# A two-block transformer on one core: the norms between the stages of the first block

## The reference, cut to what matters

```python
def rmsnorm(x, g):
    xf = x.astype(jnp.float32)
    y = xf * lax.rsqrt(jnp.mean(xf * xf, axis=-1, keepdims=True) + RMS_EPS)
    return (y * g.astype(jnp.float32)).astype(x.dtype)

for i in range(DEPTH):                                  # DEPTH = 2
    g = norm_g[i]
    f1 = swiglu(rmsnorm(h, g[0]), ffn_w_gate[i, 0], ffn_w_up[i, 0], ffn_w_down[i, 0])
    h = h + FFN_RES * rmsnorm(f1, g[1])
    hn = rmsnorm(h, g[2])
    m = neighborhood_attention(hn, ...)                 # i = 0; diff_attention for i = 1
    h = h + rmsnorm(m, g[3])
    f2 = swiglu(rmsnorm(h, g[4]), ffn_w_gate[i, 1], ffn_w_up[i, 1], ffn_w_down[i, 1])
    h = h + FFN_RES * rmsnorm(f2, g[5])
```

## Time and profile before

| | us |
|---|---|
| median of 3 runs | 2372.04 (2369.4 to 2373.62) |
| profiled execution | 2367.97 |
| its span | 2366.1 |
| PE busy in the span | 2271.9 (96%) |
| DVE busy | 1615.5 (68%) |
| ACT busy | 1040.3 (44%) |
| POOL busy | 110.4 (5%) |

### The profile page before, as it was taken

The page is one execution under the profiler, slowest core; times in us unless marked ns, Lnnn a source line. Parts: engine busy times, 40 slices in busy tenths (PEclk is TensorE's granted clock), DMA queues, the critical chain, the costliest instruction groups (busy, mean ns, idle before and its releaser), DMA issues. The chain is left out here.

```text
span 2366.1 us, 46054 instructions
## 1 busy us (share of the span) xinstructions
PE 2271.9 (96%) x18286; PEld 2132.5 (90%) x18286; DVE 1615.5 (68%) x3000; ACT 1040.3 (44%) x1688; POOL 110.4 (5%) x42
## 2 busy tenths in 40 slices
PE   7999999999999998999799998989999999999997
PEld 7999789999999887999789997989999998888886
DVE  5665567664765466766476667689889975777775
ACT  5443455443544345544363435434444444333333
POOL 0000000000000000000000000069300000000000
PEclk9999999999999999999898998999999999999999
DMA  5563434554455342456332225535444445555553
GB/s 192 171 200 118 169 109 135 177 193 147 143 174 197 122 145 81 152 187 205 113 129 73 82 82 172 167 118 169 142 141 138 142 161 169 188 194 192 191 194 133
DMA packets 99245, 361.12 MB, mean 153 GB/s; under 512 B 11496, under 2 KB 15224, under 8 KB 98944
## 3 DMA queue, kind: packets, MB, share of 16 engines
q1 hardware_dynamic: 99072, 358.64, 45.8%
HBM read 357.55 MB, written 1.05 MB: 152 GB/s over the span
## 5 line engine op out<-in xcount | busy, mean ns | idle before, releaser
L876 DVE TENSOR_TENSOR w_lo<-ring,w_hi 128x1024 fp32r<-128x1024 f32 (+1 forms) x304 | 397.6, 1308 | 241.3 <-ACT w_hi L693 241.0
L693 ACT ACTIVATE w_hi<-ring 128x1024 fp32r<-128x1024 f32 (+1 forms) x304 | 341.3, 1125 | 401.8 <-PE ps L427 364.2
L427 PE MATMUL ps<-x_hi,w_hi 128*128 128x272 f32 (+1 forms) x1664 | 488.2, 293 | 18.0 <-DVE w_lo L876 16.5
L427 PE MATMUL ps<-x_hi,w_lo 128*128 128x272 f32 (+1 forms) x1664 | 479.1, 288 | 0.0
L427 PE MATMUL ps<-x_lo,w_hi 128*128 128x272 f32 (+1 forms) x1664 | 478.4, 288 | 0.0
L427 PEld LDWEIGHTS ps<-x_hi,w_hi 128*128 128x128 f32 x1664 | 314.5, 189 | 25.2 <-issue 10.7
L427 PEld LDWEIGHTS ps<-x_lo,w_hi 128*128 128x128 f32 x1664 | 314.1, 189 | 1.0
L427 PEld LDWEIGHTS ps<-x_hi,w_lo 128*128 128x128 f32 x1664 | 314.5, 189 | 0.0
L234 ACT ACTIVATE v_gated_hi<-ring 128x1024 fp32r<-128x1024 f32 x128 | 135.9, 1062 | 214.7 <-PE ps L2863 214.0
L2650 PE MATMUL ps<-tok_hi,u_mid_hi 128*128 128x256 f32 x736 | 213.6, 290 | 1.3 <-POOL u_mid_lo L240 1.3
L2650 PE MATMUL ps<-tok_hi,u_mid_lo 128*128 128x256 f32 x736 | 208.1, 283 | 0.0
(11 more groups left out here) (479 smaller groups left out, 5029.8 us busy)
## 6 DMA issues: line engine op xcount, KB each, us to landing
ring<-in_gate_up SPq DMA_DIRECT2D x176, 512.0 KB, 3.3
ring<-in_peer_v SPq DMA_DIRECT2D x128, 512.0 KB, 3.2
ring<-in_peer_u_mid SPq DMA_DIRECT2D x92, 512.0 KB, 3.3
ring<-in_down SPq DMA_DIRECT2D x64, 704.0 KB, 4.1
ring<-in_w_in SPq DMA_DIRECT2D x46, 512.0 KB, 3.3
ring<-in_peer_u_early SPq DMA_DIRECT2D x36, 512.0 KB, 3.2
ring<-in_project SPq DMA_DIRECT2D x32, 512.0 KB, 4.1
ring<-in_na_qk SPq DMA_DIRECT2D x16, 512.0 KB, 3.8
```

The source lines that it names most:

```text
L427: mm = nc.tensor.matmul(ps[:, bank, 0:ntok], parts[left][:, slot, t * P:(t + 1) * P], rhs[right][:, k, 0:ntok], start=start and n == 0, st ...
L693: A.activation(parts[0][:, n % SLOTS, 0:width[n]], ring[:, n % SLOTS, 0:width[n]], ACT.Copy).then_inc(hi_done.sem, 1)
L876: V.tensor_tensor(parts[1][:, n % SLOTS, 0:width[n]], ring[:, n % SLOTS, 0:width[n]], parts[0][:, n % SLOTS, 0:width[n]].bitcast(F32), ALU ...
```

## The change

The boundary is computed in another way.

- **No reciprocal ahead of the products.** Instead of h + y/s (s is `std` of y), the boundary makes h' = s*h + y, which is s times the new stream. x is made of h'. Its norm cancels s, if the epsilon is multiplied by the square of s: ACT makes that square into `inv_h` (`eps_squared`), and it is added to the sum of squares. The factor s*h of tiles 0 and 1 is made by DVE (`raise_rows`, `h_raised_first`), of tiles 2 to 7 by GpSimd (`raise_rest`). Later, GpSimd multiplies h' by 1/s to bring the stream back (`lower`, `h_back`); the reciprocal that this needs (`inverse`) stands on DVE behind the last `x_lo`. At b = 6 the stream is made as before.
- **Sums of squares.** GpSimd adds the tiles of `sq` up element by element into tile 0 (`gather_y`: tiles 1 to 6; `gather_h`: the epsilon's term and tiles 1 to 7). PE multiplies by `ones` twice for a norm of y (`y_sum_most`, `y_sum_last`) and once for a norm of h, which stands behind item 3 in a feed-forward now.
- **The first tile of x.** PE starts with the products that need only `x_hi`, for three items (banks) in turn, and runs those with `x_lo` behind them.
- **Splits ahead.** At b = 0, 2, 3 and 5, two more weight items (4 and 5) are split in the boundary, and no longer in the loop. At b = 1 and 4 it stays three items.
- **keep_busy** runs 10 products, not 20.

The diff, cut to its core:

```diff
+        RAISED = range(1, 6)
+        FIRST_ROWS = 2
+        def raise_rows(eng, b, k):
+            if b == 5:
+                return eng.tensor_tensor(halves(h[:, k, :]), halves(h[:, k, :]), std[:, 0:SEQ].rearrange("p (b t) -> p b t", t=P), ALU.mult)
+            return eng.tensor_tensor(h[:, k, 0:T], h[:, k, 0:T], std[:, 0:T], ALU.mult)
+        def ahead_of(b):
+            return 3 if b in (1, 4) else 2
...
+            def y_sum_most(b):
+                pe.wait_ge(y_gathered, b)
+                nc.tensor.matmul(ps[:, 6, 0:stream(b)[1]], ones[:, :], sq[:, 0, 0:stream(b)[1]], start=True, stop=False)
+            def y_sum_last(b):
+                pe.wait_ge(y_squared, KD * b)
+                nc.tensor.matmul(ps[:, 6, 0:stream(b)[1]], ones[:, :], sq[:, KD - 1, 0:stream(b)[1]], start=False, stop=True).then_inc(y_summed, 1)
+            def h_sum(b):
+                pe.wait_ge(h_gathered, b + 1)
+                nc.tensor.matmul(ps[:, 7, 0:stream(b)[1]], ones[:, :], sq[:, 0, 0:stream(b)[1]], start=True, stop=True).then_inc(h_summed, 1)
             def keep_busy():
-                for _ in range(20):
+                for _ in range(10):
...
+            def first_side_by_side(n0, banks, ntok, b):
+                pe.wait_ge(x_hi, KD * b + 1)
+                for n, bank in enumerate(banks):
+                    pe.wait_ge(lo_done.sem, n0 + n + 1)
+                    for left in range(2):
+                        nc.tensor.matmul(ps[:, bank, 0:ntok], parts[left][:, (n0 + n) % SLOTS, 0:P], x[0][:, 0, 0:ntok], start=(left == 0), stop=False)
+                pe.wait_ge(x_lo, KD * b + 1)
+                for n, bank in enumerate(banks):
+                    nc.tensor.matmul(ps[:, bank, 0:ntok], parts[0][:, (n0 + n) % SLOTS, 0:P], x[1][:, 0, 0:ntok], start=False, stop=False)
...
-                for k in range(KD):
+                first_side_by_side(n0, (0, 1, 2), ntok, b)
+                for k in range(1, KD):
                     pe.wait_ge(x_lo, KD * b + k + 1)
                     side_by_side(n0, (0, 1, 2), k, ntok, x)
-                    if k:
-                        h_sum(b, k - 1)
-                h_sum(b, KD - 1)
                 for i in range(3, 2 * KF):
                     if i >= 6:
                         pe.wait_ge(taken, taken0 + i - 5)
                     whole_item(n0 + i, i % 6, ntok, x)
+                    if i == 3:
+                        h_sum(b)
...
-                    if side == 1 and m:
-                        y_sum(b + 1, m - 1)
-                y_sum(b + 1, KD - 1)
+                y_sum_most(b + 1)
+                y_sum_last(b + 1)
...
# ACT, boundary: behind the root of the sum for y, and ahead of the root for h
+                if b in RAISED:
+                    act.wait_ge(y_std, b)
...
+                        A.activation(inv_h[:, 0:T], std[:, 0:T], ACT.Square, scale=math.sqrt(EPS * D / P)).then_inc(eps_squared, 1)
...
-                if b in (1, 4):
-                    for n in range(n_next + 1, n_next + 4):
-                        split_hi(n)
+                for n in range(n_next + 1, n_next + 1 + ahead_of(b)):
+                    split_hi(n)
                 act.wait_ge(h_summed, b + 1)
+                if b:
+                    act.wait_ge(y_inv, b)
...
# DVE, boundary
                 def new_h(k):
-                    V.tensor_tensor(y[:, k, 0:ntok], y[:, k, 0:ntok], inv_y[:, 0:ntok], ALU.mult).then_inc(y_scaled, 1)
-                    dve.wait_ge(y_scaled, KD * (b - 1) + k + 1)
+                    if b == 6:
+                        V.tensor_tensor(y[:, k, 0:ntok], y[:, k, 0:ntok], inv_y[:, 0:ntok], ALU.mult).then_inc(y_scaled, 1)
+                        dve.wait_ge(y_scaled, k + 1)
+                    elif k < FIRST_ROWS:
+                        if b >= 2:
+                            dve.wait_ge(h_back, KD * (b - 2) + k + 1)
+                        raise_rows(V, b, k).then_inc(h_raised_first, 1)
+                        dve.wait_ge(h_raised_first, FIRST_ROWS * (b - 1) + k + 1)
+                    else:
+                        dve.wait_ge(h_raised, (KD - FIRST_ROWS) * (b - 1) + k - FIRST_ROWS + 1)
...
+                if b and b not in (1, 4):
+                    inverse()
+                for n in range(n_next + 1, n_next + 1 + ahead_of(b)):
+                    split_lo(n)
                 if b in (1, 4):
+                    inverse()
                 dve.wait_ge(h_std, b + 1)
                 V.reciprocal(inv_h[:, 0:ntok], std[:, 0:ntok]).then_inc(h_inv, 1)
...
+            def gather_y(b):
+                ntok = stream(b)[1]
+                for k in range(1, KD - 1):
+                    pool.wait_ge(y_squared, KD * (b - 1) + k + 1)
+                    if k > 1:
+                        pool.wait_ge(y_link, (KD - 3) * (b - 1) + k - 1)
+                    G.tensor_tensor(sq[:, 0, 0:ntok], sq[:, 0, 0:ntok], sq[:, k, 0:ntok], ALU.add).then_inc(y_link if k < KD - 2 else y_gathered, 1)
+            def raise_rest(b):
+                pool.wait_ge(y_std, b)
+                for k in range(FIRST_ROWS, KD):
+                    if b >= 2:
+                        pool.wait_ge(h_back, KD * (b - 2) + k + 1)
+                    raise_rows(G, b, k).then_inc(h_raised, 1)
+            def lower(b):
+                stem, ntok = stream(b)
+                pool.wait_ge(y_inv, b)
+                pool.wait_ge(x_lo, KD * (b + 1))
+                for k in range(KD):
+                    G.tensor_tensor(stem[:, k, 0:ntok], stem[:, k, 0:ntok], inv_y[:, 0:ntok], ALU.mult).then_inc(h_back, 1)
+            gather_h(0)
+            for b in range(1, 7):
+                gather_y(b)
+                if b in RAISED:
+                    raise_rest(b)
+                    gather_h(b)
+                    lower(b)
```

More of the change, by code:

```diff
@@ L502, in attention, with v_product @@
                         k = 2 * pair + t
-                        if side == 0:
+                        if side == 0 and k:
                             pe.wait_ge(x_lo, KD * b + k + 1)
-                        for tile, (t0, n) in enumerate(KEY_TILES):
-                            for term, (left, right) in enumerate(TERMS):
-                                mm = nc.tensor.matmul(ps[0:n, 3 * side + tile, :], x[left][:, k, t0:t0 + n],
-                                                      parts[right][:, (n0 + item) % SLOTS, 512 * t:512 * t + 512],
-                                                      start=(k == 0 and term == 0), stop=(k == KD - 1 and term == 2))
+                        def v_product(tile, left, right, start=False, stop=False):
+                            t0, n = KEY_TILES[tile]
+                            return nc.tensor.matmul(ps[0:n, 3 * side + tile, :], x[left][:, k, t0:t0 + n],
+                                                    parts[right][:, (n0 + item) % SLOTS, 512 * t:512 * t + 512], start=start, stop=stop)
+                        if item == 0 and k == 0:
+                            pe.wait_ge(x_hi, KD * b + 1)
+                            for tile in range(3):
+                                v_product(tile, 0, 0, start=True)
+                                v_product(tile, 0, 1)
+                            pe.wait_ge(x_lo, KD * b + 1)
+                            for tile in range(3):
+                                mm = v_product(tile, 1, 0)
+                        else:
+                            for tile in range(3):
+                                for term, (left, right) in enumerate(TERMS):
+                                    mm = v_product(tile, left, right, start=(k == 0 and term == 0), stop=(k == KD - 1 and term == 2))
                         if t == 1:
                             mm.then_inc(used, 1)
-                        if side == 0 and k:
-                            h_sum(b, k - 1)
                     if item == 3:
-                        h_sum(b, KD - 1)
+                        h_sum(b)
                     if item == 5:
@@ L671, in attention @@
                     whole_item(n0 + m, bank, ntok, o_parts)
-                    y_sum(b + 1, m - 3)
-                for m in range(KD - 3, KD):
-                    y_sum(b + 1, m)
+                y_sum_most(b + 1)
+                y_sum_last(b + 1)
                 pe.wait_ge(taken, taken0 + 3)
@@ L711, in boundary @@
                     return
+                if b in RAISED:
+                    act.wait_ge(y_std, b)
+                    if b == 5:
+                        A.activation(to_rows(inv_h[:, 0:SEQ]), by_columns(std[:, 0:SEQ]), ACT.Square, scale=math.sqrt(EPS * D / P)).then_inc(eps_squared, 1)
+                    else:
+                        A.activation(inv_h[:, 0:T], std[:, 0:T], ACT.Square, scale=math.sqrt(EPS * D / P)).then_inc(eps_squared, 1)
                 for k in range(KD):
@@ L737, in ffn @@
                 for i in range(2 * KF):
[L738 removed]
+                    if i >= 2:
+                        split_hi(n0 + i + 4)
                     j = i // 2
@@ L919, in boundary @@
```

(7 more changed lines are left out.)

59 lines of the change are left out of this document (43 added, 16 removed).

## The result

| | before | after |
|---|---|---|
| median of the runs | 2370.88 (2369.4 to 2373.62, 4 runs) | 2341.57 (2340.4 to 2343.38, 4 runs) |
| span of the profiled execution | 2366.1 | 2338.5 |
| PE busy | 2271.9 | 2235.8 |
| DVE busy | 1615.5 | 1641.7 |
| POOL busy | 110.4 | 253.8 |

The ratio is 0.9876, with a 95% interval of 0.9859 to 0.9893: 1.24% faster. The forecast was 2347, in a range of 2326 to 2362. By the profiled executions the gain is 27.6 us against the 25.2 of the sum.

A forecast was written before the change was run, and what follows sets the result against it. PE was taken as the bound, others setting the pace only in boundaries. Gains of 16.5 (sums of y), 3.9 (start), 4.8 (attention boundaries) and 0 (feed-forward boundaries) made 25.2 us, giving 2347, range 2326 to 2362.

The forecast's parts named there:

- The sums of y: Down-product stages of 6 sublayers: 36 products with `ones` at 0.46 us go off PE, 16.5 us gained.
- The price of GpSimd: A GpSimd instruction of 272 columns, shown in no earlier row, was taken to cost 0.75 us.
- The rival at 1.0 to 1.2: Boundaries: dearer GpSimd instructions lengthen DVE's chain; 2363 at 1.0, 2378 at 1.2; chances 0.04 (1.0 to 1.1), 0.04 (slower than before).
- an estimate of 0.84: GpSimd's instruction price by the skill's 4497 ns and the trace's 2.38; would shrink the gain from 25 to 19 us.
- The turns: Boundaries: of two DVE and GpSimd instructions with two SBUF inputs, one waits for the whole of the other.
- A pair: Boundaries: one DVE and one GpSimd instruction in turn cost 0.96 us, where DVE alone needs about 0.4.
- Boundaries into a feed-forward: Boundaries 2, 3, 5: first product 2.0, last `x_lo` 15.7, item 4 21.2 us behind the root; net gain about 0.
- the wait of 0.3 at item 6: Boundaries into a feed-forward: item 6 waits about 0.3 us for its `w_lo`, now behind first results, root and silu.
- Boundaries into an attention: Boundaries 1 and 4: item 4 of v starts at 21.9, before 24.3; gain 2.4 us each, 4.8 together.
- The start: At b = 0: fewer sums ahead of item 3 and no stall ahead of item 4; gain 3.9 us.
- The clock: Rival at boundaries 2, 3, 5: PE's granted clock falls, costing about 4 us at each, 2358; chance 0.12.
- a stall of 1.4: Ahead of item 4 in the kernel before: PE lost 1.4 us, which goes as splits run under item 3.

The follow-up runs named there:

- experiment 1: Kernel before with only the sums of squares of y changed: GpSimd adds squares 1 to 6, PE does 2 products with ones a sublayer; 2351.7, ratio 0.9925.
- Experiment 2: Kernel before plus 14 idle two-input GpSimd additions of 272 columns behind each root of y of boundaries 1 to 5; 2385.55, ratio 1.0067.
- experiment 4: Changed kernel with GpSimd's additions of the squares of h (b from 1) also waiting for the fifth `x_lo`; 2335.53, ratio 0.9858 to the kernel before.
- experiment 3: Kernel before plus 14 idle one-input GpSimd multiplications of 272 columns behind each root of y of boundaries 1 to 5; 2372.91, ratio 1.0011.
- experiment 6: Changed kernel with 20 idle products, not 10, behind the last sum of y; 2342.71, ratio 0.9885 to the kernel before.
- the run with 6 rows: Changed kernel with DVE raising the first 6 tiles, GpSimd 2, and GpSimd's additions for h waiting for the fifth `x_lo`; 2333.92, ratio 0.9838.
- experiment 7: Changed kernel with splits of items 4 and 5 of a feed-forward again behind the first results; 2365.28, ratio 0.9979 to the kernel before.

## Why the prediction was right

*The sums of y.* 16.5 forecast, 17.7 by ratio and 15.0 within the first block's trace in experiment 1. In the changed kernel the stages of the first three feed-forwards gave 2.9 each for 6 products, 0.48 a product and not 0.46 (18 products with `ones` are left of 96, as forecast), the last (256 tokens) 2.4, those of the attentions 2.4 and 0.1: 13.6 in all, 2.9 less than the sum had. The 0.1 is the clock, in code that the change leaves alone; over all runs this stage took 133.0 to 137.0 us. Before, it fell in the window 925 to 930 and was back at 0.81 by 935 to 940; in the changed kernel the same work met it one window longer:

```profile
900.00:905.00 5.00, 2.69 (x14) 2.32 (x13) 2.75 (x11) 3.67 (x13) 0.00 (x0) 0.61 0.00 0
905.00:910.00 5.00, 3.21 (x14) 2.65 (x12) 0.76 (x3) 2.00 (x9) 0.00 (x0) 0.50 0.00 0
910.00:915.00 5.00, 2.66 (x11) 2.26 (x12) 3.75 (x11) 0.90 (x2) 0.00 (x0) 0.50 0.00 0
915.00:920.00 5.00, 5.00 (x32) 4.94 (x32) 0.97 (x2) 1.24 (x3) 0.00 (x0) 0.68 0.00 0
```

*The price of GpSimd.* 0.75 forecast, 0.77 measured, from bounds of 0.10 and 2.38. The rival at 1.0 to 1.2 is out. The Trainium skill (GPSIMD Engine Reference, Elementwise side-by-side cycle accounting) led to an estimate of 0.84, which redone from 4497 ns and 2.38 us is 0.83. The trace's 0.77 lies midway between this and the 0.71 of the line through its own two rows, and it decides.

*The turns.* A pair was worked out at 0.96 and takes 0.92 from start to start (the earlier trace rows give 2.29 - 2.16 = 0.13 us that DVE runs ahead, where I took 0.10; with it a pair is 0.93); DVE's L972 and L977 last 0.88 to 1.00 and GpSimd's 0.94 where both work. Experiment 2 shows the mechanism alone, experiment 4 shows it from the other side. The rule of the Trainium skill (GPSIMD Engine Reference, Specifications) names contention for DVE instructions with two SBUF inputs; experiment 2 agrees, and experiment 3 adds that the price hangs on GpSimd's inputs too (16 against 2.6 us by the ratios, 16.4 against 4.7 by the boundaries of the traces).

*Boundaries into a feed-forward.* Net 0 forecast, 0.7 to 1.1 measured: the first product at 2.0 was exact, the last `x_lo` at 15.1 instead of 15.7, item 4 at 20.6 instead of 21.2, and the wait of 0.3 at item 6 didn't come. The small error is in the pair, 0.04 too dear eleven times, and in the count of pairs: GpSimd's additions waited for squares and left DVE alone (its sum of tile 5 at 584.43 took 0.43).

*Boundaries into an attention.* 2.4 forecast, 2.9 and 3.0 measured, since item 4 of v starts 21.5 behind the root and not 21.9. *The start.* 3.9 forecast, 3.35 measured. The third weight item starts at 14.70 and not 14.34 because its transfer landed later: ACT's split of it, which waits for it, starts at 12.33 and not 11.97, and in the other runs anywhere from 11.75 to 12.73. The versions that leave the start as it is in the changed kernel end it up to 1.5 us earlier, so these traces can't tell 3.35 from 3.9. GpSimd's additions put DVE into turns there as well (its last four `x_lo` take 3.77), which I hadn't counted; what that costs PE isn't shown.

*The clock.* It fell behind boundaries 2, 3 and 5 as the rival said (0.63 and 0.69 at boundary 3), but its price of 4 us each was wrong: PE waited for DVE there, and what it lost at half the clock came off its waits. That rival added two bounds that lie beside each other. It was right that a fallen clock can cost: 1.5 us each at two boundaries in experiment 6, where it fell behind the waits. Where it would fall was not worked out in the forecast, so that it fell among the waits is luck too.

*What was luck.* The first block's sum agrees to 0.1 because misses cancel (the sums of y gave 2.9 less than forecast and the start 0.55 less; boundaries 2, 3 and 5 gave 2.5 more, 1 and 4 gave 1.1 more), and the second block, the same code, gained 2.4. Why isn't shown. Over all these runs the rest of the span lies between 1198.3 and 1204.6, and the clock alone doesn't order them: in windows of 25 us the run with 6 rows spent no more time at the low clock there than the changed kernel, and took 6.1 us longer. A sum of this kind can't be trusted below about 3 us.

*What the prediction left out.* That the splits ahead are needed by the new place of the sum: without them nearly all is lost (experiment 7). It was priced as the removal of a stall of 1.4; it also covers one of 4.0 that the change itself would make.

## What to carry to other kernels

Before giving work to GpSimd, look at what DVE does at that time: instructions of both with two SBUF inputs take turns, so an addition of 0.77 us that nobody waits for still costs DVE 0.3 to 0.55. Put such work where DVE has slack or where it reads PSUM (its instructions kept their time there), and delay it past the stretch in which DVE sets the pace; a wait can be a gain. And count a moved step with what its new place makes late: the same edit can be worth 1.4 or 6 us by where the chain behind it starts.
